# Root and shift of a second LayerNorm moved from VectorE to ScalarE, in a decoder layer with mixture of experts

## The reference

```python
def layer_norm(x, g, b):
    mu = jnp.mean(xf, axis=-1, keepdims=True)
    var = jnp.mean(jnp.square(xf - mu), axis=-1, keepdims=True)
    y = (xf - mu) * lax.rsqrt(var + LN_EPS) * g + b
...
h = layer_norm(DEEPNORM_ALPHA * h + mix, ln1_g, ln1_b)
ffn = hierarchical_moe(h, ...)
h = layer_norm(DEEPNORM_ALPHA * h + ffn, ln2_g, ln2_b)
```

## Time and profile before

| | us |
|---|---|
| median of 3 runs | 431.0 |
| lowest, highest run | 430.76, 431.99 |
| profiled execution, span from first to last instruction | 432.4 |
| TensorE, VectorE, ScalarE, POOL busy in it | 410.6, 186.8, 114.5, 83.1 |

### The profile page before, as it was taken

One profiled execution on the slowest core, in us unless ns is written; L12 is line 12 of the kernel. 1 busy time (PEld: TensorE's weight loads), 2 busy tenths in 40 slices (PEclk: granted clock), 3 DMA queues, 4 the chain that ended last, 5 costly groups with the idle time before them and its releaser, 6 DMA issues.

```text
span 432.4 us, 6542 instructions
## 1 busy us (share of the span) xinstructions
PE 410.6 (95%) x2578; PEld 277.1 (64%) x2578; DVE 186.8 (43%) x368; ACT 114.5 (26%) x185; POOL 83.1 (19%) x111
## 2 busy tenths in 40 slices
PE   6999999999999999989999999999999999788883
PEld 5888877888888888955555555556555655454331
DVE  1578722499957467855322122212222221111077
ACT  3524376973122002310111111111111111003211
POOL 2201000000000001011332333233223322110124
PEclk8999999999999999998999999999999999898997
DMA  8766340230369999999999999999999999999584
GB/s 266 220 222 208 126 146 28 93 97 31 114 218 420 425 418 420 422 407 378 403 418 413 418 411 412 417 414 411 418 416 417 418 418 416 418 417 416 196 352 194
DMA packets 37377, 139.11 MB, mean 322 GB/s; under 512 B 5107, under 2 KB 17427, under 8 KB 25062
## 3 DMA queue, kind: packets, MB, share of 16 engines
q1 hardware_dynamic: 31184, 126.89, 73.7%
q0 software_dynamic: 6144, 11.84, 7.5%
q10 hardware_dynamic: 22, 0.02, 0.0%
HBM read 134.41 MB, written 12.58 MB: 340 GB/s over the span
## 4 chain that ended last, share of the span: by engine, by line
PE 82%; DMA 11%; DVE 5%; issue 1%; ACT 0%; SPq 0%; DVEq 0%; POOLq 0%
PE bank L1102 24%; PE bank L915 12%; PE bank L917 12%; PE bank L916 12%; PE bank L1131 11%; DMA wgu_first<-in_exp_w_up 7%; PE bank L1092 3%; PE bank L1122 3%; DMA xg<-h_rows,x_rows 2%; DVE stats L1585 1%; DMA pair_y<-y_pairs 1%; PE bank L1012 1%; DMA raw<-in_w_in 1%; PE bank L1024 1%; PE bank L975 1%; PE bank L898 1%
## 5 line engine op out<-in xcount | busy, mean ns | idle before, releaser
L1102 PE MATMUL bank<-wgu,xTg 128*64 128x256 f32 x736 | 87.7, 392 | 3.3 <-DMA wgu<-in_exp_w_up 2.4
L1102 PEld LDWEIGHTS bank<-wgu,xTg 128*64 128x64 f32 x736 | 52.6, 141 | 31.0 <-issue 3.6
L915 PE MATMUL bank<-xT_hi,w_hi 128*128 128x512 f32 x160 | 63.2, 395 | 1.8 <-DVE xT_lo L1242 1.8
L916 PE MATMUL bank<-xT_lo,w_hi 128*128 128x512 f32 x160 | 62.8, 392 | 0.0
L917 PE MATMUL bank<-xT_hi,w_lo 128*128 128x512 f32 x160 | 62.8, 392 | 0.0
L1541 DVE TENSOR_TENSOR hid<-hid,bank 64x256 f32<-64x256 f32 x32 | 13.5, 423 | 105.8 <-ACT hid L841 105.7
L681 POOL DMA_INDIRECT y_pairs<-ys,y_rows x32 | 32.5, 1016 | 134.0 <-PE bank L1092 103.6
L841 ACT ACTIVATE hid<-bank 64x256 f32<-64x256 f32 x32 | 12.1, 377 | 130.8 <-PE bank L1102 130.7
L1131 PE MATMUL bank<-wdn,hidT 128*64 128x512 f32 x192 | 45.3, 593 | 0.0
L1219 DVE TENSOR_TENSOR w_lo<-raw,w_hi 128x2048 fp32r<-128x2048 f32 x12 | 27.5, 2289 | 26.9 <-ACT w_hi L755 26.8
L676 POOL DMA_INDIRECT xg<-h_rows,x_rows x31 | 31.5, 1015 | 31.4 <-issue 19.0
(11 more groups left out here) (253 smaller groups left out, 497.2 us busy)
## 6 DMA issues: line engine op xcount, KB each, us to landing
wgu<-in_exp_w_gate SPq DMA_DIRECT2D x24, 1024.0 KB, 19.4
wgu<-in_exp_w_up SPq DMA_DIRECT2D x24, 1024.0 KB, 22.4
wdn<-in_exp_w_down SPq DMA_DIRECT2D x24, 1024.0 KB, 22.4
raw<-in_w_in SPq DMA_DIRECT2D x9, 1024.0 KB, 5.2
raw<-in_w_out SPq DMA_DIRECT2D x4, 1024.0 KB, 5.0
wgu_spare<-in_exp_w_gate SPq DMA_DIRECT2D x4, 1024.0 KB, 22.1
wgu_spare<-in_exp_w_up SPq DMA_DIRECT2D x4, 1024.0 KB, 24.3
wdn_first<-in_exp_w_down SPq DMA_DIRECT2D x4, 1024.0 KB, 24.8
```

What stands on the lines that cost most here:

```text
L915: pe.matmul(dst, a_hi, b_hi, start=start, stop=False)
L916: pe.matmul(dst, a_hi, b_lo, start=False, stop=False)
L1102: mm = pe.matmul(psum[2 + b][BLOCK * which:BLOCK * which + BLOCK, 0:F], xTg[b][:, j, h * BLOCK:(h + 1) * BLOCK], wgu[s][:, which, k, :], s ...
```

## The change

The small constant of the normalisation gets a tile of its own, eps, which POOL sets at the start. ScalarE adds it as the bias of its square root, reading the variance directly. The shift is made by ScalarE too, in two copies: mean * rstd, and that times -1. VectorE's two small operations go (the first for four tiles, the second for three). ScalarE waits once for eps, ahead of its loop over the tiles.

```diff
+        eps = sb("eps", [P, 1])
...
             pool.memset(held[:, :], 1.0).then_inc(pool_chain, 1)
+            pool.memset(eps[:, :], LN_EPS).then_inc(eps_set, 1)
...
+            act.wait_ge(eps_set, 1)
             for t in range(TT):
                 act.wait_ge(var2_ready, t + 1)
-                act.activation(rstd[:, t:t + 1], rstd[:, t:t + 1], ACT.Sqrt).then_inc(dev2_ready, 1)
+                act.activation(rstd[:, t:t + 1], moments[:, t, 1:2], ACT.Sqrt, bias=eps[:, 0:1]).then_inc(dev2_ready, 1)
                 if t < TT - 1:
 
-                    act.wait_ge(moments2_ready, t + 1)
+                    act.wait_ge(rstd2_ready, t + 1)
+                    act.activation(shift[:, t:t + 1], moments[:, t, 0:1], ACT.Copy, scale=rstd[:, t:t + 1]).then_inc(shift_ready, 1)
+                    act.wait_ge(shift_ready, 2 * t + 1)
+                    act.activation(shift[:, t:t + 1], shift[:, t:t + 1], ACT.Copy, scale=-1.0).then_inc(shift_ready, 1)
+                    act.wait_ge(shift_ready, 2 * t + 2)
                     act.activation(pair_y[t][1][:, 0:H], z_of(t, 0), ACT.Identity,
                                    bias=shift[:, t:t + 1], scale=rstd[:, t:t + 1]).then_inc(normed2, 1)
...
                 v.wait_ge(dve, chain[0])
-                link(v.bn_aggr(moments[:, t, :], stats[:, t, :, :]))
-                v.tensor_scalar(rstd[:, t:t + 1], moments[:, t, 1:2], LN_EPS, None, ALU.add).then_inc(var2_ready, 1)
+                v.bn_aggr(moments[:, t, :], stats[:, t, :, :]).then_inc(var2_ready, 1)
+                v.wait_ge(var2_ready, t + 1)
...
                 v.wait_ge(dev2_ready, t + 1)
-                link(v.reciprocal(rstd[:, t:t + 1], rstd[:, t:t + 1]))
-                if t < TT - 1:
-                    v.tensor_scalar(shift[:, t:t + 1], moments[:, t, 0:1], rstd[:, t:t + 1], -1.0, ALU.mult, ALU.mult).then_inc(moments2_ready, 1)
+                v.reciprocal(rstd[:, t:t + 1], rstd[:, t:t + 1]).then_inc(rstd2_ready, 1)
+                v.wait_ge(rstd2_ready, t + 1)
```

More of the change, by code:

```diff
@@ L297, in hybrid_moe_layer @@
         ident_done = sem("ident_done")
+        eps_set = sem("eps_set")
         const_pool = sem("const_pool")
@@ L376, in hybrid_moe_layer @@
         dev2_ready = sem("dev2_ready")
-        moments2_ready = sem("moments2_ready")
+        shift_ready = sem("shift_ready")
+        rstd2_ready = sem("rstd2_ready")
         normed2 = sem("normed2")
```

## The result

The changed kernel takes 432.62 us (median of 22 runs, 431.33 to 434.27); the kernel before, in 22 runs, 431.53 us (430.76 to 434.97). The ratio is 1.0026 with a 95% interval of 1.0015 to 1.0038: 1.1 us slower (0.65 to 1.64).

The account below looks back on a forecast made before the run. The prediction took the issue of tile 2's store, with the stores queued behind it, to bound the end. Lateness 0.56 + 0.31 = 0.87 us on the median 431.0 gave 431.9 us, 0.20% slower; range 430.8 to 432.6.

Parts of the forecast that it names:

- The load goes onto the path: ScalarE, second normalisation: the root's table load waits for tile 0's variance, making tile 0's reciprocal 0.96 us late.
- VectorE's returns of 0.13 and 0.07 a tile: VectorE, second normalisation: removing two small operations shrinks the reciprocal's lateness from 0.96 us in tile 0 to 0.36 in tile 3.
- the 0.75 us from reciprocal to normalising: ScalarE: two dependent copies for the shift lengthen this way from 0.44 to 0.75 us, 0.31 more.
- tile 2's store 0.89 late for 0.87: SP queue: tile 2's store was forecast 0.87 us late, 0.56 from the reciprocal plus 0.31 from the copies, moving the end equally.
- the three stores without a gap: End of kernel: tile 2's store and tile 3's two halves stay back to back, so the end moves by 0.87 us.
- The pointer operand: ScalarE's root and first copy: a per-partition operand makes each take 0.20 to 0.29 us; 0.29 was taken.
- The load ahead: Rival: the root's table load still runs right after the branch; end moves by -0.08 us, about 430.9 us; chance 0.13.
- VectorE as the end: Rival: VectorE sets the kernel's end, as the chain says, and wins the whole 0.67 us: 430.3 us; chance 0.03.
- The stall beyond the load: Rival: the table switch stalls ScalarE in tile 0 beyond its load, 1.28 us more, giving 433.2 us; chance 0.04.
- the chain's last piece: End of the chain of waits, from 428.87 us: read as the store queue waiting for VectorE's L1602.
- 431.0 + 0.87 = 431.9: Whole time: the 0.87 us shift put on the before kernel's median of 431.0 us, 0.20% slower.
- TensorE's sums 0.1 us short of being a hold: Second normalisation: sums end at 425.50 us, VectorE due at tile 3's last half at 425.57, a tenth of a microsecond later.

Follow-up runs that it names:

- load_ahead: Changed kernel with the wait for the constant taken early in ScalarE's queue, so the first root carries one wait; ratio to before 1.0011 (0.9990 to 1.0032).
- load_twice: Changed kernel plus an unused exponential after tile 0's variance wait, forcing a second table load before the root; ratio to before 1.0058 (1.0035 to 1.0080).
- waits_swapped: Changed kernel with the first root's two waits in the other order, variance then constant; 15.9 us from tile 0's aggregate to the end, no ratio given.

## Why the prediction was right in its mechanism and a little low

*The load.* "The load goes onto the path" held: 0.29 us behind the aggregate's start, the root 1.30 behind the load, the reciprocal at 416.42, which is 418.40 on the clock of the before profile; 418.42 was forecast. Two kernels put the load ahead again and lost the delay in the tail; one brought it about with a wait alone; one added a second load and its price came on top. That cause is shown for the tail. In whole times load_ahead by itself is too coarse (1.0011, 0.9990 to 1.0032); what shows it there is that the three kernels with a load behind the wait lie at 1.0026 to 1.0058, no interval holding 1, and the timed kernels with the load ahead at 0.9994 to 1.0011, every interval holding 1.

*The way to the end.* VectorE's returns of 0.13 and 0.07 a tile, the 0.75 us from reciprocal to normalising (422.60 to 423.35), tile 2's store 0.89 late for 0.87, the three stores without a gap: each as forecast. The pointer operand took the upper value, 0.29.

*The rivals.* The load ahead: refuted by the first line of the timeline. VectorE as the end: refuted, since tile 3's last store came only some 0.4 us later, counted from the aggregate, while the end came 0.9 later. The table says it more broadly: in the eleven profiles that store tile 2 whole, the end comes 4.4 us after the issue of that store, within 0.1 us (tail less the column beside it), while it comes 2.6 to 3.3 us after the issue of the last one. The prediction read the chain's last piece as the store queue's; it is VectorE's own, and the chain ends at 429.53, before any of the last three stores had landed. So it never spoke about the stores, and there was less to argue against than the prediction thought. The stall beyond the load: refuted by load_twice.

*The step that failed* is the one that put the shift on the median: "431.0 + 0.87 = 431.9". The base was the median of three runs, and over 22 runs it is 431.53. From there 0.87 gives 432.4; measured were 432.62, two hundredths above the range, which ended at 432.6. The term for the change was 0.87, and the ratio gives 1.1 (0.65 to 1.64), which holds it. The mechanism was right; the term that was off is the base. The range had 0.7 us above the forecast for placement or scatter, and the base alone took 0.53 of it.

A weaker place stood behind it: I took the tail of before, 15.9 us, for fixed, with TensorE's sums 0.1 us short of being a hold. In two other profiles of the same instructions they were one, and against those the changed kernel's 16.7 is 0.1 to 0.5 us longer, not 0.8. That 0.89 met 0.87 so closely is in part luck with the profile. The mean of the three, 16.2, leaves 0.5 us for the change, a little under the lower end of what the times say. The other profiles narrow this. A lead of the sums over the aggregate of 1.01 us cost 0.33 us against the first profile and one of 0.61 cost 0.74, so by an estimate from these two each tenth under about 1.35 us costs a tenth. Over all 14 profiles the lead was 1.34 us or more in ten and 0.61 to 1.01 in four. By that the usual tail of before is 15.9, its mean 16.0, and the change costs some 0.7 us on average, inside the interval of the times. Whether the rest, up to 1.1, is scatter or something ahead of the tail stays open: the executions differ by up to 3.8 us in when tile 0's aggregate starts (412.69 to 416.49), and a profile of each doesn't settle some tenths.

## What to carry to other kernels

Before you add a wait in front of a ScalarE function that may need a table load, look where the load stands in the trace and what it waits for: a wait that has long been fulfilled can still push another one in front of the load. Here it helped to take such a wait on an earlier instruction (load_ahead), or to write it last (waits_swapped). And at the end of a kernel look at the DMA view before believing the chain, which stops at the last operation of an engine: with three stores back to back in one queue the end here followed the issue of the first of them, not that of the last.

## What the runs showed that was not expected

TensorE's granted clock drops to its lower level (1.2 GHz, 0.5 in the profile) for a few microseconds, one to four times in an execution ahead of the tail, and where it does differs from one to the next. In the profile of before one such stretch lay on the last expert's gate, after TensorE had waited 2.02 us for its weights; in the changed kernel one lay on the sums of the first normalisation's output, after a wait of 2.45 us for their load. The changed kernel's sums, then the two stretches, before and changed, in the columns of the earlier trace rows (a clock of 0.57 is the mean of the stretch):

```profile
401.84 8.80 PE L1202 MATMUL bank<-h,diag 128*128 128x512 f32 x16 [2.45 <-DMA h<-h_rows]
```

```profile
393.00:397.00 4.00, 3.31 (x16) 1.94 (x18) 0.00 (x0) 1.41 (x5) 0.65 (x1) 0.57 1.01 414
403.00:407.00 4.00, 4.00 (x6) 1.54 (x5) 0.00 (x0) 0.00 (x0) 0.00 (x0) 0.57 0.27 82
```

In load_ahead the same 16 matmuls ran at the full clock, behind a wait of the same length:

```profile
401.79 7.11 PE L1202 MATMUL bank<-h,diag 128*128 128x512 f32 x16 [2.45 <-DMA h<-h_rows]
```

So the wait alone doesn't say where the clock falls, and what does stays open. The difference is 1.7 us, more than the whole change is worth, and one reason why single spans can't be compared here.
